# Part of the low-order weights made by a negated copy and an adding SBUF-to-SBUF transfer

## The reference

```python
def swiglu(x, w_up, w_down):
    g, u = jnp.split(x @ w_up, 2, axis=-1)
    return (jax.nn.silu(g) * u) @ w_down
...
h = h + 0.5 * rms_norm(swiglu(rms_norm(h, ffn1_pre[l]), ffn1_up[l], ffn1_down[l]), ffn1_post[l])
...
h = h + 0.5 * rms_norm(swiglu(rms_norm(h, ffn2_pre[l]), ffn2_up[l], ffn2_down[l]), ffn2_post[l])
```

## Time and profile before

| | |
|---|---|
| time, median of 3 runs | 2388.61 us (2387.86 to 2389.59) |
| span of the profiled execution | 2387.2 us |
| busy: PE, DVE, ACT, POOL | 2370.4, 1644.4, 1207.4, 200.2 us |
| TensorE clock granted, mean | 0.999 |
| one up strip | 41.49 us |
| up strips in the program | 20 |

### The profile page before, as it was taken

The page is one execution under the profiler, slowest core; times in us unless marked ns, Lnnn a source line. Parts: engine busy times, 40 slices in busy tenths (PEclk is TensorE's granted clock), DMA queues, the critical chain, the costliest instruction groups (busy, mean ns, idle before and its releaser), DMA issues.

```text
span 2387.2 us, 34469 instructions
## 1 busy us (share of the span) xinstructions
PE 2370.4 (99%) x10667; PEld 1955.8 (82%) x10667; DVE 1644.4 (69%) x1905; ACT 1207.4 (51%) x1444; POOL 200.2 (8%) x392
## 2 busy tenths in 40 slices
PE   9999999999999999999999999999999999999998
PEld 7888888888887888888888888888788888888887
DVE  5999999974456655655545545555799999996444
ACT  5555555554445454454544444444655555555443
POOL 1212112110000000000000000000021212111000
PEclk9999999999999999999999999999999999999999
DMA  7666666666656565565666666655566666666664
GB/s 234 219 212 207 219 208 226 209 221 184 204 173 192 158 185 172 161 189 158 200 188 197 190 195 192 194 182 186 176 210 222 215 214 205 218 211 225 192 194 155
DMA packets 265731, 470.99 MB, mean 197 GB/s; under 512 B 21056, under 2 KB 54512, under 8 KB 265296
## 3 DMA queue, kind: packets, MB, share of 16 engines
q1 hardware_dynamic: 252752, 453.04, 60.6%
q0 software_dynamic: 12752, 17.24, 2.3%
q10 hardware_dynamic: 176, 0.07, 0.0%
HBM read 456.64 MB, written 2.10 MB: 192 GB/s over the span
## 4 chain that ended last, share of the span: by engine, by line
PE 96%; DVE 2%; issue 1%; DMA 1%; ACT 0%; DVEq 0%; POOL 0%; ACTq 0%; SPq 0%; POOLq 0%
PE acc L684 24%; PE acc L686 24%; PE acc L685 24%; PE acc L775 5%; PE acc L776 5%; PE acc L777 5%; PE bank L775 2%; PE bank L776 2%; PE bank L777 2%; PE bank L705 1%; DVE w_lo L1437 1%; DVE h L1501 0%; DVE xT_lo L1448 0%; PE bank L1011 0%; PE bank L945 0%
## 5 line engine op out<-in xcount | busy, mean ns | idle before, releaser
L1437 DVE TENSOR_TENSOR w_lo<-w_raw,w_hi 128x1024 fp32r<-128x1024 f32 (+1 forms) x856 | 1011.1, 1184 | 633.0 <-ACT w_hi L1112 628.8
L1112 ACT ACTIVATE w_hi<-w_raw 128x1024 fp32r<-128x1024 f32 (+1 forms) x856 | 880.4, 1031 | 1055.1 <-PE acc L686 810.6
L684 PE MATMUL acc<-w_hi,xT_hi 128*128 128x512 f32 x1584 | 622.5, 393 | 3.6 <-DVE xT_lo L1448 2.4
L686 PE MATMUL acc<-w_hi,xT_lo 128*128 128x512 f32 x1584 | 616.9, 389 | 0.0
L685 PE MATMUL acc<-w_lo,xT_hi 128*128 128x512 f32 x1584 | 616.7, 389 | 0.0
L684 PEld LDWEIGHTS acc<-w_hi,xT_hi 128*128 128x128 f32 x1584 | 297.4, 188 | 67.6 <-DVE xT_lo L1448 3.3
L686 PEld LDWEIGHTS acc<-w_hi,xT_lo 128*128 128x128 f32 x1584 | 297.3, 188 | 62.6
L685 PEld LDWEIGHTS acc<-w_lo,xT_hi 128*128 128x128 f32 x1584 | 297.5, 188 | 60.0
L684 PE MATMUL acc<-w_hi,act_hi 128*128 128x512 f32 x704 | 274.3, 390 | 1.5 <-DVE act_lo L1470 1.5
L686 PE MATMUL acc<-w_hi,act_lo 128*128 128x512 f32 x704 | 273.9, 389 | 0.0
L685 PE MATMUL acc<-w_lo,act_hi 128*128 128x512 f32 x704 | 273.9, 389 | 0.0
(11 more groups left out here) (206 smaller groups left out, 2128.9 us busy)
## 6 DMA issues: line engine op xcount, KB each, us to landing
w_raw<-in_ffn_up_dram SPq DMA_DIRECT2D x352, 512.0 KB, 4.2
w_raw<-in_ffn_down_dram SPq DMA_DIRECT2D x176, 512.0 KB, 4.7
w_raw<-in_w_gate_dram SPq DMA_DIRECT2D x96, 512.0 KB, 4.1
w_raw<-in_w_in_dram SPq DMA_DIRECT2D x72, 512.0 KB, 3.7
w_raw<-in_w_in_dram SPq DMA_DIRECT2D x128, 256.0 KB, 3.0
w_raw<-in_w_ret_out_dram SPq DMA_DIRECT2D x32, 512.0 KB, 4.8
w_raw<-in_w_out_dram SPq DMA_DIRECT2D x32, 512.0 KB, 4.8
act_raw<-blocks POOLq DMA_DIRECT2D x352, 32.0 KB, 3.8
```

Of the source, the lines that this page charges most:

```text
L684: pe.matmul(pair[m][:, :], xh, wh, start=(first and kk == 0), stop=False)
L686: mm = pe.matmul(pair[m][:, :], xl, wh, start=False, stop=(last and kk == KG - 1))
L1112: act.activation(w_hi[:, s, cols], w_raw[:, s, cols], ACT.Copy).then_inc(w_rounded, 1)
L1437: dve.tensor_tensor(w_lo[:, s, cols], w_raw[:, s, cols], w_hi[:, s, cols].bitcast(f32), ALU.subtract).then_inc(w_split, 1)
```

## The change

In each up strip the groups 7, 11 and 14 no longer get `w_lo` from DVE. ACT, right after rounding such a group into `w_hi`, writes minus the same rounded value into `w_lo` (a copy with scale -1). POOL waits for that, and issues a transfer from `w_raw` to `w_lo` that adds to what it finds there, which leaves raw - rounded. The slot's `w_raw` is free for the next load when this transfer has landed, and PE waits for the landing too.

```diff
+DMA_REST = (7, 11, 14)
...
             def load(sec, i, n, src):
                 s = n % SLOTS
+                if by_dma(sec, n - SLOTS):
+                    wait_lo_landed(sp, sec, i, n - SLOTS)
+                    sp.sem_inc(slot_free, 1)
                 sp.wait_ge(w_split, group(sec, i, n) + 1)
                 sp.dma_start(slot(s), src).then_inc(w_landed[s], 16)
...
                     sp.wait_ge(t_summed, 3 * (quad(f, i, NQUAD - 1) + 1))
                     sp.sem_inc(slot_summed, 1)
+                    for n in range(2 * GD - SLOTS, 2 * GD):
+                        if n in DMA_REST:
+                            wait_lo_landed(sp, f"up{f}", i, n)
+                            sp.sem_inc(slot_free, 1)
...
+            def rest_by_dma(f, i):
+
+                for j, n in enumerate(DMA_REST):
+                    s = n % SLOTS
+                    pool.wait_ge(hi_negated, len(DMA_REST) * (NST * f + i) + j + 1)
+                    pool.sem_inc(rest_begun, 1)
+                    pool.dma_start(w_lo[:, s, :].bitcast(f32), w_raw[:, s, :], accum_op=ALU.add).then_inc(lo_landed[j], 16)
...
-            with pool.Fori(0, NUP) as p:
-                turn_hidden(0, p)
+            with pool.Fori(0, NST) as i:
+                turn_hidden(0, i)
+                rest_by_dma(0, i)
+            turn_hidden(0, NST)
...
+            def wait_weights(sec, i, n):
+
+                if by_dma(sec, n):
+                    pe.wait_ge(w_rounded, group(sec, i, n) + 1)
+                    wait_lo_landed(pe, sec, i, n)
+                pe.wait_ge(w_split, group(sec, i, n) + 1 + SLOTS)
...
                     act.activation(w_hi[:, s, cols], w_raw[:, s, cols], ACT.Copy).then_inc(w_rounded, 1)
+                    if by_dma(sec, ahead):
+                        act.activation(w_lo[:, s, cols], w_raw[:, s, cols], ACT.Copy, scale=-1.0).then_inc(hi_negated, 1)
...
                 s, cols = n % SLOTS, w_cols(sec, n + SLOTS)
+                if by_dma(sec, n + SLOTS):
+                    return
+                groups = 2 if by_dma(sec, n + SLOTS + 1) else 1
                 dve.wait_ge(w_rounded, group(sec, i, n + SLOTS) + 1)
-                dve.tensor_tensor(w_lo[:, s, cols], w_raw[:, s, cols], w_hi[:, s, cols].bitcast(f32), ALU.subtract).then_inc(w_split, 1)
+                dve.tensor_tensor(w_lo[:, s, cols], w_raw[:, s, cols], w_hi[:, s, cols].bitcast(f32),
+                                  ALU.subtract).then_inc(w_split, groups)
```

More of the change, by code:

```diff
@@ L320, in hybrid_trunk @@
         slot_summed = sem("slot_summed")
+        slot_free = sem("slot_free")
         t_rounded = sem("t_rounded")
@@ L330, in hybrid_trunk @@
         hid_split = sem("hid_split")
+        hi_negated = sem("hi_negated")
+        rest_begun = sem("rest_begun")
+        lo_landed = [sem(f"lo_landed{r}") for r in range(len(DMA_REST))]
         def group(sec, i, n):
@@ L449, in t_pair, with by_dma, wait_lo_landed @@
             return a[:, T_SLOT[j], 2 * pair:2 * pair + 2, :]
+        def by_dma(sec, n):
+            return sec in ("up0", "up1") and n in DMA_REST
+        def wait_lo_landed(eng, sec, i, n):
+            eng.wait_ge(lo_landed[DMA_REST.index(n)], 16 * (NST * ("up0", "up1").index(sec) + i + 1))
         T_AT = {ng - 3 + pair: (j, pair) for j, (ng, nu, k) in enumerate(QUADS) for pair in range(2)}
@@ L660, in _ @@
             rsqrt("pre2", rs_pre[:, 2, :])
-            with pool.Fori(0, NUP) as p:
-                turn_hidden(1, p)
+            with pool.Fori(0, NST) as i:
+                turn_hidden(1, i)
+                rest_by_dma(1, i)
+            turn_hidden(1, NST)
             wait_strip_read(pool, "up1", NST - 1, 1)
@@ L676, in products @@
                 if tiles[0] == 0:
-                    pe.wait_ge(w_split, group(sec, i, n) + 1 + SLOTS)
+                    wait_weights(sec, i, n)
                 for kk in range(KG):
```

## The result

The changed kernel takes 2589.75 us (median of 4 runs, 2589.05 to 2593.79) against 2388.49 us before: ratio 1.0845, 95% interval 1.0831 to 1.086. It is slower by 201 us. The forecast was 2587 us. The profiled execution spans 2587.3 us, 200.1 more than the earlier trace rows.

What follows compares the result with a forecast made beforehand. PE was taken as the bound in up strips, with late adding transfers stretching each strip. Losses of 99 us per layer, 198 in two, took 2387.2 to 2585, plus 1.4 for runs: 2587 us; range 2470 to 2700 (about 0.82).

Steps and rivals of the forecast that it cites:

- PE is the bound, relief is worth 0: Up strips: PE waits for nobody, so taking 68 us of subtractions off DVE gives back 0.
- The unknown L: Time from an adding transfer's issue on POOL to its landing: estimated 5.4 us, ends 3.2 and 8.1.
- Two passes: Adding transfer fetches source and destination, so it costs like twice the bytes: 2 x 1.63 us within the 5.4.
- The loop P = 41.0 + 2L: Shortest strip, through SP, ACT, DVE and POOL but not PE: 51.8 us at L = 5.4 against 41.49, +10.3.
- Rival D, the short loop: Strip's end has unseen slack, only direct stalls before groups 7 and 11 stay: 5.5 per strip, +110, 2499 us; chance 0.10.
- The wait at the strip's end: SP's wait for group 14's landing stands ahead of all loads of the next strip; load 0' lands at 17.9 + L.
- bandwidth is not the first limit: DMA queues in an up strip: share rises from 0.67 to at most some 0.9 of 41.49 us.
- Where PE waits: Stalls per up strip: 2.4 us before group 11, about 2 before group 4', near 6 before group 7'.
- The stall before group 4': Next strip's group 4: PE waits about 2 us because DVE is late.
- The clock costs 0: Clock may fall in every strip, but PE's slack of some 4 us absorbs a loss of 1.5 to 2.5 us.
- The sum, 198 per program: Both layers, 99 us each: 3.1 first strip, 92.7 for nine distances, 2.4 last strip, 1 down stage.
- rival B: Adding transfer as fast as a copy, L 3.2 to 4.8, same loop: +84 to +175, 2473 to 2564 us; chance 0.25.

Runs made afterwards that it cites:

- the run with the relief alone: Changed kernel with the low parts of groups 7, 11 and 14 left out: no DVE subtraction, negated copy or adding transfer; 2388.5 us, ratio 1.0002.
- the second run: Changed kernel where ACT makes the negated copies but DVE subtracts again and no adding transfer is issued; 2389.65 us, ratio 1.0005.
- the run with the filled gaps: Changed kernel plus 17 unused matmuls (3.9 us) at the start of each later strip, where PE waits for gate_sb; 2595.0 us.
- group 7 alone: Changed kernel with the change applied to group 7 only (DMA_REST = (7,)); 2465.1 us, +77.
- group 14 alone: Changed kernel with the change applied to group 14 only (DMA_REST = (14,)); 2508.4 us, +120.
- a quarter of the bytes: Changed kernel, group 7's transfer issued before the turned block, SP's wait for 14 moved to its slot's load, transfers adding 256 of 1024 columns; 2426.2 us.
- the 32 us of group 11: Changed kernel with the change applied to group 11 only (DMA_REST = (11,)); 2420.5 us, +32.

## Why the prediction was right, and where it was not

*PE is the bound, relief is worth 0.* Right, shown by the run with the relief alone (1.0002), and for ACT's copies by the second run.

*The unknown L.* The estimate was 5.4, measured 4.5. Two passes was right: adding takes 2.7 us of the DMA engines and copying 1.3. Both terms were a little too large. Two passes at 1.63 are 3.26 and measure 2.7; the fixed part, (3.5 - 1.63) of a load from HBM plus 0.3 for POOL, is 2.2, and 4.5 - 2.7 = 1.8 is left for it here, 2.9 - 1.3 = 1.6 with a copy. That the landings lie 1.6 apart, as the 1.63 from the earlier trace rows, is partly chance: 1.4 is the second pass, and POOL's longer issue may be the rest. The Trainium skill (DMA: Bandwidth & Descriptors, Anatomy of one DMA) gives 3.2 us by its fit, an estimate which counts the bytes once: close to the 2.9 of the copy, and not to the 4.5 of the addition. The same page of the Trainium skill says that an accumulating transfer reads its destination and writes it later (Rules for kernel authors); the doubled queue time agrees.

*The loop P = 41.0 + 2L.* The length and the slope are right at two values of L: 50.0 and 46.97 us measured in the strips shown, 50.0 and 46.8 worked out. At the larger L most strips are 0.2 to 1.1 us longer than that. Rival D, the short loop, gives 3.7 us more per strip at L = 4.5 and falls. But the middle of the loop is less simple than I put it. The wait at the strip's end is not the one carrier: when it is moved, load 0' and the adding transfer share the queues and arrive nearly as late. The step "bandwidth is not the first limit" holds for the changed kernel, whose loads still land after 4.2 us in the median of the first layer's strips (3.4 to 7.5), but not beyond it: the mean share of 0.72 says nothing of four transfers issued within 2 us, as in the run with SP's wait moved.

*Where PE waits.* Before groups 7 and 11, as said, but for less: mostly 1.4 and 0.6 to 1.8 us in the first layer, not near 6 and 2.4. The stall before group 4' is in truth one before group 0', 4.0 us for `gate_sb`: the next strip's first product needs the accumulators that DVE reads at the strip's end, a wait on `acc_read` that I left out. The length of the strip did not depend on it, since DVE's work there is in the loop either way.

*The clock costs 0.* Right for this kernel: in the run with the filled gaps nothing came back, and strips at 0.93 and 0.97 are equally long. It holds only while PE is off the loop. With group 7 alone a fall goes with 1.6 us more in a strip, and with group 14 alone its absence gives back 1.5. The Trainium skill (TensorE: Matmul & The Clock Gate, Why this matters for your kernels) warns of such gaps. That the clock falls behind them the traces of all three kernels bear out; that it costs time, those of the two with one group and not that of the changed kernel.

*The sum, 198 per program.* That 200.1 was measured is in part luck. L = 4.5 lies in the range of rival B (3.2 to 4.8, times up to 2564), not in that of the forecast (4.8 to 7). With the L that was measured, my sum gives 2.2 (group 7) + 9 x 8.5 (the distances) + 1.5 (group 11) + 1 (down stage) = 81 per layer, 163 in two, and 2551 us: some 38 less than came. The L that was too large hid two things that the sum did not have.

First, the nine distances from POOL's first block to its tenth grow by 84.6 and 88.6 us in the two layers, not by 76.5, because of POOL's pauses and some strips of 51 us. (The 92.7 forecast came from the larger L.) Second, everything outside these distances, which the sum had at 3.1 + 2.4 + 1 = 6.5 a layer, costs 11.5 and 15.3. The step that fails here is the layer's end: the last strip was to lose 2.4 us, but the distance from its block to the one before grows by 10 us, as in any strip (522.39 to 576.82, where it was 438.45 to 482.82). The down stage then waits for that hidden block: 13.7 us in two waits on `act_lo`, 1.5 before. I had treated that end as free.

What stays open: which of ACT, DVE or the queues makes the 38 us that are left with a quarter of the bytes, how much of the 32 us of group 11 is sharing with loads rather than its own 4.5 us; and what POOL's pauses are. None was taken apart further.

## What to carry to other kernels

When an engine off the critical path is relieved, cost the replacement by latency, not by work: where does it stand in its queue, what buffer does it hold, and who is in order behind the wait for it. Add the whole loop up once round, from a buffer's release to its next release; its length predicted this kernel although the engine that it starved was not in it. And before a wait is moved, ask what goes out at the same moment once it is gone: here a load and an adding transfer of the same size, with two more loads beside them, took 7.8 and 8.0 us, where they took 4.2 and 4.5 with less around them.

## What the runs showed of the hardware

- An SBUF-to-SBUF transfer of 512 KB that adds takes 2.7 us of all sixteen DMA engines and 4.5 us to its landing when little else is under way; a copy of the same bytes takes 1.3 and 2.9. POOL is busy for 0.90 us to issue one.
- After waits of 3.2 us (group 14 alone) and 4.05 us (changed kernel, at 259.6) the granted clock was 0.50, the lower of its two levels, and a matmul of 512 columns started every 0.43 us and not 0.227. With group 7 alone the length of the wait did not settle it: waits of 2.8 and 2.2 us were followed by a fall (strips of 45.5 us at 0.96), waits of 2.1 and 2.6 were not (43.9 at 1.00).
- POOL pauses for 1.6 to 3 us between two of its issues. In all fourteen traces, whatever the strip and the time, the first such pause comes after its 135th transfer; two more follow in the second layer. Before the change, two strips' blocks start 44.6 and then 38.4 us apart there, and nobody notices. In the changed kernel the same pause stands in the loop, and that strip takes 53.8 us, some 3.5 more than its neighbours, with nothing regained:

```profile
368.19 3.81 POOL L633 DMA_DIRECT2D act_raw<-blocks  x7 [22.86 <-DVE blocks L1678]
372.19 3.76 POOL L633 DMA_DIRECT2D act_raw<-blocks  x7 [0.18 <-issue]
378.72 1.05 POOL L633 DMA_DIRECT2D act_raw<-blocks  x2 [2.77 <-issue]
```
